# Split matmul products with the moving operand and the bank's columns taken from last to first

## The reference

```
q = (ht @ w_q); s1, s2 = products with two sets of 128 sub-keys
v1, i1 = top_k(s1, 16); v2, i2 = top_k(s2, 16)
top, pos = top_k(v1[:, None] + v2[None, :], 16); gate = softmax(top)
act = gelu(einsum('td,thkd->thk', h, expert_u[ec]))
y = einsum('thk,thkd->td', gate * act, expert_v[ec])
```

## Time and profile before

| | us |
|---|---|
| median of three runs | 2432.15 |
| profiled execution | 2441.18 |
| its span, first to last instruction | 2439.4 |
| mean granted TensorE clock | 0.984 |
| TensorE busy | 2361.4 |
| VectorE busy | 1714.9 |
| ScalarE busy | 1130.5 |
| GpSimd busy | 148.5 |

### The profile page before, as it was taken

The page is one execution under the profiler, slowest core; times in us unless marked ns, Lnnn a source line. Parts: engine busy times, 40 slices in busy tenths (PEclk is TensorE's granted clock), DMA queues, the critical chain, the costliest instruction groups (busy, mean ns, idle before and its releaser), DMA issues. The chain is left out here.

```text
span 2439.4 us, 39506 instructions
## 1 busy us (share of the span) xinstructions
PE 2361.4 (97%) x15756; PEld 2179.5 (89%) x15756; DVE 1714.9 (70%) x2863; ACT 1130.5 (46%) x1631; POOL 148.5 (6%) x205
## 2 busy tenths in 40 slices
PE   5989999999999999999999999999999999999998
PEld 5879898889999999889899889999999888998998
DVE  7979887676666666678988676556766566655665
ACT  4542355444444444565155444445444423545544
POOL 0000352000000000000055000000000000000000
PEclk8989999999999999999999999999999999999999
DMA  9365445786666666434534686655555523343553
GB/s 357 139 229 167 149 133 168 267 292 241 233 241 232 240 233 223 151 113 150 180 123 137 201 308 207 217 203 189 189 189 189 190 78 104 130 150 134 184 190 104
DMA packets 133556, 460.67 MB, mean 189 GB/s; under 512 B 15152, under 2 KB 16432, under 8 KB 132912
## 3 DMA queue, kind: packets, MB, share of 16 engines
q1 hardware_dynamic: 133424, 458.90, 55.1%
HBM read 445.73 MB, written 13.11 MB: 188 GB/s over the span
## 5 line engine op out<-in xcount | busy, mean ns | idle before, releaser
L1680 DVE TENSOR_TENSOR ring_lo<-ring,ring_hi 128x1024 fp32r<-128x1024 f32 x421 | 507.1, 1223 | 392.6 <-ACT ring_hi L1591 392.6
L315 PE MATMUL banks<-normed_lo,ring_hi 128*128 128x256 f32 x2096 | 593.3, 283 | 1.2 <-DVE ring_lo L357 0.8
L316 PE MATMUL banks<-normed_lo,ring_hi 128*128 128x256 f32 x2096 | 589.1, 281 | 0.0
L317 PE MATMUL banks<-normed_lo,ring_lo 128*128 128x256 f32 x2096 | 589.0, 281 | 0.0
L1591 ACT ACTIVATE ring_hi<-ring 128x1024 fp32r<-128x1024 f32 x421 | 435.9, 1056 | 170.1 <-PE banks L342 156.9
L340 PE MATMUL banks<-ring_hi,work_lo 128*128 128x512 f32 x1024 | 399.4, 390 | 8.2 <-DVE work_lo L1701 4.6
L315 PEld LDWEIGHTS banks<-normed_lo,ring_hi 128*128 128x128 f32 x2096 | 396.8, 189 | 6.7 <-issue 1.3
L317 PEld LDWEIGHTS banks<-normed_lo,ring_lo 128*128 128x128 f32 x2096 | 400.5, 191 | 0.0
L341 PE MATMUL banks<-ring_lo,work_lo 128*128 128x512 f32 x1024 | 399.1, 390 | 0.0
L342 PE MATMUL banks<-ring_hi,work_lo 128*128 128x512 f32 x1024 | 399.0, 390 | 0.0
L316 PEld LDWEIGHTS banks<-normed_lo,ring_hi 128*128 128x128 f32 x2096 | 395.4, 189 | 3.4
(11 more groups left out here) (395 smaller groups left out, 3677.5 us busy)
## 6 DMA issues: line engine op xcount, KB each, us to landing
ring<-wstream SPq DMA_DIRECT2D x716, 512.0 KB, 3.3
arena<-wstream SPq DMA_DIRECT2D x96, 512.0 KB, 5.3
spill<-one_hots SPq DMA_DIRECT2D x44, 256.0 KB, 4.2
rstd<-spill SPq DMA_DIRECT2D x16, 256.0 KB, 3.8
pool_and_keys<-spill SPq DMA_DIRECT2D x14, 256.0 KB, 3.9
routes<-spill SPq DMA_DIRECT2D x14, 256.0 KB, 4.8
residual<-xT SPq DMA_DIRECT2D x1, 1024.0 KB, 7.8
arena<-mixconst SPq DMA_DIRECT2D x2, 512.0 KB, 4.4
```

The lines of the kernel that those rows point to most:

```text
L315: pe.matmul(dst, w_hi[:, o], hi[:, k, :], start=(k == 0), stop=False)
L316: pe.matmul(dst, w_hi[:, o], lo[:, k, :], start=False, stop=False)
L317: mm = pe.matmul(dst, w_lo[:, o], hi[:, k, :], start=False, stop=(k == KD - 1))
L1680: dve.tensor_tensor(RING_LO[:, u % SLOTS, :], RING[:, u % SLOTS, :], RING_HI[:, u % HIGHS, :].bitcast(F32), ALU.subtract).then_inc(S("spli ...
```

## The change

In all split products but one group, the moving operand is read from its last column to its first, and the output's columns are written from last to first, so every result lands where it did. The stationary operand stays. The group of L2462 to L2464 (values of the cross attention) and all plain fp32 matmuls are as they were. `mirrored` is a new helper.

```diff
+        def mirrored(view):
+
+            return view[:, ::-1]
+
 def unit_product(pe, dst, u, hi, lo):
...
-                pe.matmul(dst, w_hi[:, o], hi[:, k, :], start=(k == 0), stop=False)
-                pe.matmul(dst, w_hi[:, o], lo[:, k, :], start=False, stop=False)
-                mm = pe.matmul(dst, w_lo[:, o], hi[:, k, :], start=False, stop=(k == KD - 1))
+                pe.matmul(mirrored(dst), w_hi[:, o], hi[:, k, ::-1], start=(k == 0), stop=False)
+                pe.matmul(mirrored(dst), w_hi[:, o], lo[:, k, ::-1], start=False, stop=False)
+                mm = pe.matmul(mirrored(dst), w_lo[:, o], hi[:, k, ::-1], start=False, stop=(k == KD - 1))
...
 def unit_wide(pe, u, hi, lo, first, last, done=None):
...
-                    pe.matmul(dst, hi[:, t], w_hi[:, o], start=first, stop=False)
-                    pe.matmul(dst, hi[:, t], w_lo[:, o], start=False, stop=False)
-                    mm = pe.matmul(dst, lo[:, t], w_hi[:, o], start=False, stop=last)
+                    pe.matmul(mirrored(dst), hi[:, t], mirrored(w_hi[:, o]), start=first, stop=False)
+                    pe.matmul(mirrored(dst), hi[:, t], mirrored(w_lo[:, o]), start=False, stop=False)
+                    mm = pe.matmul(mirrored(dst), lo[:, t], mirrored(w_hi[:, o]), start=False, stop=last)
```

More of the change, by code:

```diff
@@ L325, in unit_spread @@
                 dst = PS[:, 4 + k // 2, (k % 2) * T:(k % 2 + 1) * T]
-                pe.matmul(dst, w_hi[:, o], hi, start=(first and k % 2 == 0), stop=False, skip_group_check=True)
-                pe.matmul(dst, w_hi[:, o], lo, start=False, stop=False, skip_group_check=True)
-                mm = pe.matmul(dst, w_lo[:, o], hi, start=False, stop=last, skip_group_check=True)
+                pe.matmul(mirrored(dst), w_hi[:, o], mirrored(hi), start=(first and k % 2 == 0), stop=False, skip_group_check=True)
+                pe.matmul(mirrored(dst), w_hi[:, o], mirrored(lo), start=False, stop=False, skip_group_check=True)
+                mm = pe.matmul(mirrored(dst), w_lo[:, o], mirrored(hi), start=False, stop=last, skip_group_check=True)
                 if done and k % 2 and k < KD - 1:
@@ L493, in unit_group @@
                     w_hi, w_lo = parts_of(u)
-                    pe.matmul(dst, w_hi[:, o], H_HI[:, k, :], start=(first and k == 0), stop=False, skip_group_check=True)
-                    pe.matmul(dst, w_hi[:, o], H_LO[:, k, :], start=False, stop=False, skip_group_check=True)
-                    mm = pe.matmul(dst, w_lo[:, o], H_HI[:, k, :], start=False, stop=(k == KD - 1),
+                    pe.matmul(mirrored(dst), w_hi[:, o], H_HI[:, k, ::-1], start=(first and k == 0), stop=False, skip_group_check=True)
+                    pe.matmul(mirrored(dst), w_hi[:, o], H_LO[:, k, ::-1], start=False, stop=False, skip_group_check=True)
+                    mm = pe.matmul(mirrored(dst), w_lo[:, o], H_HI[:, k, ::-1], start=False, stop=(k == KD - 1),
                                    skip_group_check=True)
@@ L840, in _ @@
                             dst = PS[:, 2 + i, 0:T]
-                            pe.matmul(dst, w_hi[:, o], MIX_HI[:, k, :], start=(k == 6), stop=False, skip_group_check=True)
-                            pe.matmul(dst, w_hi[:, o], MIX_LO[:, k, :], start=False, stop=False, skip_group_check=True)
-                            mm = pe.matmul(dst, w_lo[:, o], MIX_HI[:, k, :], start=False, stop=(k == 3),
+                            pe.matmul(mirrored(dst), w_hi[:, o], MIX_HI[:, k, ::-1], start=(k == 6), stop=False, skip_group_check=True)
+                            pe.matmul(mirrored(dst), w_hi[:, o], MIX_LO[:, k, ::-1], start=False, stop=False, skip_group_check=True)
+                            mm = pe.matmul(mirrored(dst), w_lo[:, o], MIX_HI[:, k, ::-1], start=False, stop=(k == 3),
                                            skip_group_check=True)
@@ L1252, in ahead @@
                                     else:
-                                        pe.matmul(dst, WK_LO[:, u % 2, o], H_HI[:, k, :], start=(k == 0), stop=False)
-                                        pe.matmul(dst, WK_LO[:, u % 2, o], H_LO[:, k, :], start=False, stop=False)
-                                        mm = pe.matmul(dst, RING_LO[:, u % SLOTS, o], H_HI[:, k, :],
+                                        pe.matmul(mirrored(dst), WK_LO[:, u % 2, o], H_HI[:, k, ::-1], start=(k == 0), stop=False)
+                                        pe.matmul(mirrored(dst), WK_LO[:, u % 2, o], H_LO[:, k, ::-1], start=False, stop=False)
+                                        mm = pe.matmul(mirrored(dst), RING_LO[:, u % SLOTS, o], H_HI[:, k, ::-1],
                                                        start=False, stop=(k == KD - 1))
@@ L2030, in out_group @@
                         dst = PS[:, 2 + i, 0:T]
-                        pe.matmul(dst, w_hi[:, o], MIX_HI2[:, k, :], start=(k == 0), stop=False, skip_group_check=True)
-                        pe.matmul(dst, w_hi[:, o], MIX_LO[:, k, :], start=False, stop=False, skip_group_check=True)
-                        mm = pe.matmul(dst, w_lo[:, o], MIX_HI2[:, k, :], start=False, stop=(k == KD - 1),
+                        pe.matmul(mirrored(dst), w_hi[:, o], MIX_HI2[:, k, ::-1], start=(k == 0), stop=False, skip_group_check=True)
+                        pe.matmul(mirrored(dst), w_hi[:, o], MIX_LO[:, k, ::-1], start=False, stop=False, skip_group_check=True)
+                        mm = pe.matmul(mirrored(dst), w_lo[:, o], MIX_HI2[:, k, ::-1], start=False, stop=(k == KD - 1),
                                        skip_group_check=True)
@@ L2537, in _ @@
                         dst = PS[:, 4 + i, 0:T]
-                        pe.matmul(dst, w_hi[:, o], OX_HI[:, k, :], start=(k == 0), stop=False)
-                        pe.matmul(dst, w_hi[:, o], OX_LO[:, k, :], start=False, stop=False)
-                        mm = pe.matmul(dst, w_lo[:, o], OX_HI[:, k, :], start=False, stop=(k == KD - 1))
+                        pe.matmul(mirrored(dst), w_hi[:, o], OX_HI[:, k, ::-1], start=(k == 0), stop=False)
+                        pe.matmul(mirrored(dst), w_hi[:, o], OX_LO[:, k, ::-1], start=False, stop=False)
+                        mm = pe.matmul(mirrored(dst), w_lo[:, o], OX_HI[:, k, ::-1], start=False, stop=(k == KD - 1))
                         if k == KD - 1:
```

## The result

The changed kernel takes 2464.24 us (median of four runs, 2462.74 to 2467.58) against 2433.64 us for the kernel before in the same comparison: the ratio is 1.0128, with a 95% interval of 1.0105 to 1.015. It is slower by about 31 us, clear of noise. The time lies inside the range that was given, but on the side that I held less likely than no difference.

What follows compares the result with a forecast made beforehand. The prediction took TensorE, busy 97% of the span, to bound the kernel. Every term of the change was put at 0, so the forecast was the median before, 2432 us, with a range of 2398 to 2484 us.

Steps and rivals of the forecast that it cites:

- no difference: Whole kernel: the change leaves the time as it was, 2424 to 2440 us; likeliest case, chance 0.42.
- What bounds the kernel: Whole kernel: TensorE, busy 97% of the span, sets the time, nearly number of matmuls times start-to-start pace.
- Instructions, dependencies, weight loads, the bank's readers: Whole kernel: none added, removed or moved, load order kept, banks read only after a group's last matmul; cost nothing.
- The write to the bank: Output columns of the changed matmuls: descending writes cost 0, within the same bounds as the read.
- The moving read: 9408 matmuls of 256 and 3072 of 512 columns: descending reads cost 0, between 126 us gained and 1506 us lost.
- Rival 2: Changed matmuls on TensorE: descending stream meets the weight load once more per matmul; +48 us, 2480 us, chance 0.22.
- Rival 1: 256-column matmuls: stream and weight load no longer meet, quick pace wins; 32 us gained, 2400 us, chance 0.26.
- Rival 3: Changed matmuls: descending reads or writes go at half rate; 1506 us more, 3938 us, chance 0.10.
- rival 4: Changed access patterns: turned back before reaching the chip, so no difference; counted as part of the forecast, without its own chance.

Runs made afterwards that it cites:

- read_only: Kernel before, with the moving operand read last to first in all the change's groups but the bank written first to last: 2463.95 us, ratio 1.014.
- write_only: Kernel before, with the bank written last to first in the change's groups but the moving operand read first to last: 2432.84 us, ratio 1.0006.
- place_forth: Kernel before, all reads ascending, without the pad ahead of the work tile, shifting expert activations and weights' high parts: 2465.87 us, beside 2442.32 us for before.
- short_loads_forth: Kernel before, reads ascending, 32 stationary columns instead of 128 in all `unit_wide` matmuls except each layer's first and last pair: 2430.71 us.
- blocks_back64: Kernel before, with all split products read and written in 64-column (256-byte) blocks from last block to first, each block ascending: 2431.85 us.
- blocks_back16: Kernel before, with all split products read and written in 16-column (64-byte) blocks from last block to first, each block ascending: 2469.0 us.
- short_loads_back: Kernel before, with `unit_wide` reading last to first and 32 stationary columns instead of 128 there, except each layer's first and last pair: 2457.9 us.
- both widths runs: Kernel before, second and third of each three `unit_wide` matmuls cut from 512 to 384 or 448 columns: 2350.99 us ascending, 2355.53 us with `unit_wide` descending.
- all384_forth: Kernel before, reads ascending, 384 of each 512 columns in all `unit_wide` matmuls except each layer's first and last pair: 2286.66 us.
- loads32_forth: Kernel before, reads ascending, 32 stationary columns instead of 128 in the second of each three `unit_wide` matmuls: 2442.4 us.

## Why the prediction was wrong

- *What bounds the kernel*: right. TensorE's extra time came out in the whole one to one, as its 97% had said: 20 us and 11 us for the parts, 31 us together.
- *Instructions, dependencies, weight loads, the bank's readers*: right, nothing there moved. *The write to the bank*: right, 0 (1.0006).
- *The moving read*: this is the step that failed. The bounds of 126 us less and 1506 us more held, and the value inside them, 0 by "the same instruction in the same place", was wrong. Its term measures 6.6 ns on each of 3072 matmuls of 512 columns, 20 us, and 11 us on the 256-column ones, by the loss of their quick pace. The row that I took as nearest shares everything with the changed one but the order in which SBUF is read, and that order was the change. The paragraph before had found that at full clock something beside the array's clock holds the matmul back (113.3 and 226.7 ns, where half of the half-clock figure is 106.5 and twice that 213), and it named the reading of the moving operand as one of three candidates. With that found, 0 for the read had no ground. read_only (2463.95 us) and write_only (2432.84 us) show that it is the reading.
- *Rival 2* had the right side and 48 us for 31. Its mechanism, a further meeting with the weight load, is refuted by the short loads: 233.3 ns with whole and with short ones. Its prices were off both ways: 2.3 ns for 6.6 on 512 columns, 4.3 ns for 1.2 (11 us over 9408) on 256. The objection that I raised, that the 512-column form knows one state only, was void: it has at least 226.7, about 232 and 233.3 ns, as place_forth and short_loads_forth show. That the time fell between no difference and this rival, inside the range, is luck as to the mechanism.
- *Rival 1* would have been fed by the quick pace; the opposite happened, the quick pace is lost. I had read it as set by how a unit starts, "and that isn't touched". It needs reads that ascend at least within 256 bytes: 957 quick threes in blocks_back64, none in blocks_back16 and none in the change. And it needs the places: one of 3136 threes in place_forth. That the place alone doesn't choose the pace stands, but a change of place is enough to lose the quick one.
- *Rival 3*, half rate, and *rival 4*, a pattern turned back before it reaches the chip, fall: the paces of the read groups changed, and none by more than some per cent.

What stays open: what in the read path makes the order of 64-byte blocks within 256 bytes matter, and by what the ascending stream chooses between its paces. That the place and the length of the weight loads (or the number of stationary columns) have a say in it is shown; how is not. Also open is the gain that this hints at: had the 256-column matmuls of both expert stages the quick pace, 2 x 672 x 13.3 ns = 18 us would be saved. No version that reaches this with whole results was run; the change itself is to be undone.

## What to carry to other kernels

In this kernel the pace at full clock was longer than half of the pace at half clock, and the order in which the moving operand was read counted: descending order cost time, descending blocks of 64 bytes cost as much, and descending blocks of 256 bytes, each ascending in itself, cost nothing. A matmul whose paces stand like that is a reason to test the read order before calling it free; that it is always the read that holds such a matmul back isn't shown. A bank can be written from its last column to its first at no cost. Measure such an edit from start to start of the matmuls, since the rows of the trace overlap. And don't cost a changed access pattern at nothing because the instruction is the same.

## What the runs showed of the hardware

- A float32r matmul of 512 moving columns took 226.7 ns ascending, 233.3 ns descending, and 266.7 ns with the columns turned inside each 64 bytes (read and written so). With the granted clock at half, 256 columns took 213 ns in either direction, and no loss was seen.
- Fewer stationary columns, and so shorter weight loads beside it, made the ascending stream slower, not faster: 226.7 ns with 128, 231.3 to 231.9 ns with 32. The descending stream stayed at 233.3 ns.
- The pace of 256-column matmuls (113.3 or 117.8 ns) is a state that outlives units. In the expert stages it was slow beside 512-column matmuls with whole loads (before) and with descending reads and short loads (short_loads_back), and quick beside ascending ones with short loads (short_loads_forth); beside narrower ones it was quick too (both widths runs, all384_forth), and with one short load of three in the second layer's stage only (loads32_forth). One stage, the second feed-forward, was quick in some traces (276 ns a row) and slow in others (281 ns) with the same ascending reads.
